# Modulation products in halves of the contraction, at twenty places instead of ten

## What is computed

```python
for l in range(DEPTH):
    mod = (jax.nn.silu(c_ctx) @ ada_w[l] + ada_b[l])[None, None, :]     # ada_w: (2, 1024, 6 * 1024)
    x, st = trunk_layer(x, mod, P, l, None)

def trunk_layer(x, mod, P, l, ctx):
    sh1, sc1, g1, sh2, sc2, g2 = jnp.split(mod, 6, axis=-1)
    h = rms_norm(x, P['norm_mix'][l]) * (1 + sc1) + sh1
    ...                                   # l = 0: even_mixer (mLSTM scan and MLA attention), l = 1: odd_mixer
    x = x + g1 * out
    h = rms_norm(x, P['norm_ffn'][l]) * (1 + sc2) + sh2
    x = x + g2 * hier_moe(h, P, l)
```

## Time and profile before

| | us |
|---|---|
| median of three runs | 1317.55 (1315.46 to 1319.56) |
| the profiled execution | 1329.77 |
| its span | 1327.7 |
| TensorE busy | 1190.6 (90%) |
| VectorE, ScalarE, GpSimd busy | 489.2, 350.7, 115.6 |
| TensorE waits in 100 to 330 us: for `in_ada_w` | 12.7, in 5 waits |
| mean rate from HBM over the span | 263 GB/s |

### The profile page before, as it was taken

One profiled execution on the slowest core, in us unless ns is written; L12 is line 12 of the kernel. 1 busy time (PEld: TensorE's weight loads), 2 busy tenths in 40 slices (PEclk: granted clock), 3 DMA queues, 4 the chain that ended last, 5 costly groups with the idle time before them and its releaser, 6 DMA issues. The chain is left out here.

```text
span 1327.7 us, 17676 instructions
## 1 busy us (share of the span) xinstructions
PE 1190.6 (90%) x6730; PEld 686.5 (52%) x6730; DVE 489.2 (37%) x1074; ACT 350.7 (26%) x750; POOL 115.6 (9%) x142
## 2 busy tenths in 40 slices
PE   5999987998999999878899999899889899988884
PEld 3555563346973333333456555888879533333323
DVE  3004473245261111100555984678832511110014
ACT  2101514245222111110324434442432211111111
POOL 1600000000011111110000000200000111111100
PEclk9899998989989999899998999799989899998897
DMA  9972398773569999997513310010274899999971
GB/s 363 315 290 61 126 327 321 286 287 136 243 244 385 417 412 418 409 404 295 204 64 127 107 52 0 2 34 2 100 261 178 310 374 418 410 414 399 392 282 48
DMA packets 87929, 329.15 MB, mean 248 GB/s; under 512 B 19184, under 2 KB 25498, under 8 KB 66977
## 3 DMA queue, kind: packets, MB, share of 16 engines
q1 hardware_dynamic: 72560, 297.40, 57.7%
q0 software_dynamic: 15280, 30.56, 6.6%
HBM read 320.04 MB, written 29.53 MB: 263 GB/s over the span
## 5 line engine op out<-in xcount | busy, mean ns | idle before, releaser
L1020 PE MATMUL psum<-wide,ring 128*128 128x384 f32 x704 | 241.3, 503 | 4.2 <-ACT wide L1764 1.9
L1020 PEld LDWEIGHTS psum<-wide,ring 128*128 128x128 f32 x704 | 165.7, 239 | 71.6 <-issue 9.7
L1395 PE MATMUL psum<-arena 128*64 128x512 f32 x568 | 157.1, 609 | 15.6 <-DMA arena<-in_moe_w_up 10.0
L1020 PE MATMUL psum<-ring,wide 128*128 128x512 f32 (+2 forms) x336 | 119.6, 515 | 0.0
L2511 DVE TENSOR_TENSOR arena<-arena,psum 128x256 f32<-128x256 f32 x34 | 14.3, 422 | 276.8 <-ACT arena L1921 276.8
L1395 PEld LDWEIGHTS psum<-arena 128*64 128x64 f32 x568 | 50.3, 140 | 116.6 <-issue 115.5
L1921 ACT ACTIVATE arena<-psum 128x256 f32<-128x256 f32 x34 | 13.1, 384 | 309.8 <-PE psum L1395 309.8
L1395 PE MATMUL psum<-ring,arena 128*64 128x512 f32 x320 | 77.9, 643 | 11.1 <-DMA ring<-in_moe_w_up 11.1
L1020 PEld LDWEIGHTS psum<-ring,wide 128*128 128x128 f32 x336 | 59.6, 198 | 53.5 <-issue 52.6
L1395 PE MATMUL psum<-wide,arena 128*64 128x512 f32 x160 | 72.2, 605 | 0.0
L2524 DVE TENSOR_SCALAR arena<-psum,share 128x512 f32<-128x512 f32 x34 | 25.5, 751 | 122.0 <-PE psum L1421 121.9
(11 more groups left out here) (544 smaller groups left out, 1673.4 us busy)
## 6 DMA issues: line engine op xcount, KB each, us to landing
ring<-in_ada_w SPq DMA_DIRECT2D x23, 2048.0 KB, 10.0
arena<-in_moe_w_gate SPq DMA_DIRECT2D x24, 1024.0 KB, 11.7
arena<-in_moe_w_up SPq DMA_DIRECT2D x24, 1024.0 KB, 20.5
arena<-in_moe_w_down SPq DMA_DIRECT2D x24, 1024.0 KB, 23.2
ring<-in_moe_w_gate SPq DMA_DIRECT2D x20, 1024.0 KB, 16.6
ring<-in_moe_w_up SPq DMA_DIRECT2D x20, 1024.0 KB, 19.6
ring<-in_moe_w_down SPq DMA_DIRECT2D x20, 1024.0 KB, 21.4
ring<-in_w_in_odd SPq DMA_DIRECT2D x7, 2048.0 KB, 8.3
```

What stands on the lines that cost most here:

```text
L1020: ins = mm(out, lhs(k), rhs(k), start=(k == 0), stop=(k == n - 1))
L1395: ins = mm(psum[half, 2 + s, :].rearrange("p (w f) -> p w f", w=2), hg[s][:, k, half], gate_up_of(UNITS[q][h], k), start=(k == 0), stop=(k ...
```

## The change

A part's `mod_rows` becomes two jobs, one for each half of the contraction. A half needs one load and frees its slot when it is computed. The four column groups are now four quarters of the output columns (every fourth column, `quarter::4`) in place of two halves times even and odd, with 256 columns a matmul. `mod` sums the two halves in PSUM, with `pick` eight columns wide, in two accumulated steps. ScalarE copies each half by itself. The twenty halves of the ten parts have twenty places, and the last `mod` a further one: new ones are at `tb` 1, at `N2` and `CU` of the scan, at `qf` 0, 2, 4 and 6, and at `pT` (0,4), (1,4), (2,0) and (2,4). The first two parts, ahead of the projections, are split as well.

```diff
 def mods_beside():
-    places = [("N1", 2 * pair, 0) for pair in range(3)] + [("cqT", 0), ("hmT", 0), ("qf", 3), ("qR", 0), ("vv", 0)]
-    places += [("pT", c, h) for c, h in ((0, 0), (1, 0), (1, 4))]
+    places = [("tb", 1), ("N1", 0, 0), ("CU", 0, 0), ("N1", 2, 0), ("N2", 2, 0), ("CU", 2, 0), ("N1", 4, 0), ("cqT", 0), ("hmT", 0)]
+    places += [("qf", h) for h in range(0, MLA_H, 2)] + [("qR", 0), ("vv", 0)]
+    places += [("pT", c, h) for c, h in ((0, 0), (0, 4), (1, 0), (1, 4), (2, 0), (2, 4))]
     parts = MOD_PARTS[MODS_FIRST:]
...
+    halves = [("mod_rows", *part, half) for part in parts for half in range(2)]
+    def at(n):
+        whole = [("mod", *parts[n // 2 - 1])] if n and n % 2 == 0 else []
+        return whole + halves[n:n + 1]
...
 def plan_weights():
     def ada(parts):
-        return [("ada", (l, i, half), ("mod_rows", l, i)) for l, i in parts for half in range(2)]
+        return [("ada", (l, i, half), ("mod_rows", l, i, half)) for l, i in parts for half in range(2)]
...
             def modulate(name, l, i, half=0):
+                b = issue(name, l, i, half) if name == "mod_rows" else issue(name, l, i)
                 if name == "mod_rows":
-                    if (l, i) in MOD_PARTS[1:MODS_FIRST]:
+                    if (l, i) in MOD_PARTS[1:MODS_FIRST] and half == 0:
                         keep_busy(b, 3)
-                    w = [weight("ada", (l, i, half)).rearrange("p (k n) -> p k n", k=4) for half in range(2)]
+                    w = weight("ada", (l, i, half)).rearrange("p (k n) -> p k n", k=4)
                     for k in range(4):
-                        for parity in range(2):
-                            for half in range(2):
-                                at_ = 32 * (2 * parity + half)
-                                ins = mm(b[at_:at_ + 32, :], sil[:, 4 * half + k, :], w[half][:, k, parity::2],
-                                         start=(k == 0), stop=(k == 3), tile_position=(0, at_))
+                        for quarter in range(4):
+                            at_ = 32 * quarter
+                            ins = mm(b[at_:at_ + 32, 0:2 * P], sil[:, 4 * half + k, :], w[:, k, quarter::4],
+                                     start=(k == 0), stop=(k == 3), tile_position=(0, at_))
                     ready(ins)
                 else:
-                    pe.wait_ge(*taken("mod_rows", l, i))
-                    for m in range(4):
-                        ins = mm(b[:, 4 * m:4 * m + 4], mod_rows[:, m * P:(m + 1) * P], pick, start=True, stop=True)
+                    for half in range(2):
+                        pe.wait_ge(*taken("mod_rows", l, i, half))
+                    for m in range(2):
+                        for half in range(2):
+                            at_ = (2 * half + m) * P
+                            ins = mm(b[:, 8 * m:8 * m + 8], mod_rows[:, at_:at_ + P], pick, start=(half == 0), stop=(half == 1))
                     ready(ins)
```

More of the change, by code:

```diff
@@ L93 @@
 C_SEL = C_ROT + ROPE
-C_PLACE = C_SEL + 4
+C_PLACE = C_SEL + 8
 C_HOME = C_PLACE + EXPERTS
@@ L136, in const_table @@
     c[:, C_ROW:C_ROW + 2 * TILES] = row + P * np.arange(2 * TILES)[None, :] - NO_ROW
-    for parity in range(2):
-        for half in range(2):
-            for cond in range(2):
-                c[32 * (2 * parity + half) + cond, C_SEL + 2 * parity + cond] = 1.0
+    for quarter in range(4):
+        for cond in range(2):
+            c[32 * quarter + cond, C_SEL + 2 * quarter + cond] = 1.0
     half, nf = ROPE // 2, ROPE // 4
@@ L188, in plan_jobs @@
     jobs += norm(0)
-    jobs += [(name, l, i) for l, i in MOD_PARTS[:MODS_FIRST] for name in ("mod_rows", "mod")]
+    jobs += [job for l, i in MOD_PARTS[:MODS_FIRST] for job in (("mod_rows", l, i, 0), ("mod_rows", l, i, 1), ("mod", l, i))]
     jobs += [("qT", h) for h in range(4)] + [("kT", h) for h in range(4)]
@@ L1070, in _ @@
             for l, i in MOD_PARTS[:MODS_FIRST]:
-                modulate("mod_rows", l, i)
+                for half in range(2):
+                    modulate("mod_rows", l, i, half)
                 modulate("mod", l, i)
@@ L1147, in _ @@
             for c in range(TILES):
+                beside("tb", c)
                 even_rows("tb", c, w, IN_EVEN - 5 * 512)
@@ L1161, in _ @@
                         two_heads(b, half, lambda h: ST[d][:, tok(h)], lambda h: vN[:, c, h, :])
+                beside("N2", 2 * pair, 0)
                 if sequence:
@@ L1170, in _ @@
                             two_heads(b, half, lambda h: qT[:, h, tok(c)], lambda h: mlC[:, 1, d, h, :])
+                beside("CU", 2 * pair, 0)
                 if moves_on:
@@ L1758, in _ @@
             for l, i in MOD_PARTS[:MODS_FIRST]:
-                mod_row_copy(l, i)
+                for half in range(2):
+                    mod_row_copy(l, i, half)
             act.wait_ge(S("normal"), KD)
@@ L1808, in _ @@
             beside("N1", 0, 0)
+            beside("CU", 0, 0)
             head_squares(0, 1)
-            beside("N1", 2, 0)
-            beside("N1", 4, 0)
+            for place_ in (("N1", 2, 0), ("N2", 2, 0), ("CU", 2, 0), ("N1", 4, 0)):
+                beside(*place_)
             head_squares(2, 2)
@@ L2116, in beside @@
             def beside(*job):
-                for name, l, i in parts_at.get(job, []):
+                for name, *part in parts_at.get(job, []):
                     if name == "mod":
-                        modulation(l, i)
+                        modulation(*part)
             def norm(n):
```

28 lines of the change are left out of this document (13 added, 15 removed).

## The result

| | before | changed |
|---|---|---|
| median of 3 runs, us | 1317.55 (1315.46 to 1319.56) | 1357.08 (1354.15 to 1365.64) |
| profiled execution, us (span) | 1329.77 (1327.7) | 1354.15 (1352.1) |
| start of the first projection, us | 40.18 | 44.39 |
| start of `qR`, us | 249.27 | 269.06 |
| start of the output projection, us | 321.86 | 350.64 |

The ratio is 1.027, with a 95% interval of 1.021 to 1.033 (the two medians alone give 1.030). The prediction was 1310.5 us, range 1303 to 1338: the sign is wrong, and the time lies outside the range. What happened is rival 1, beyond even the worst time that was worked out for it (near 1350).

The account below looks back on a forecast made before the run. TensorE's waits for `in_ada_w` weights (12.7 us) and slow clock (4.2 us) were taken as the bound. Start -1.8, middle -5.2 and attention 0 gave -7.0 us: 1310.5 from 1317.55, range 1303 to 1338 (likeliest case 1304 to 1315).

Parts of the forecast that it names:

- rival 1: All halves: reading at stride four costs a factor of 1.55, 3.1 us a half, total 1330.5 us; chance 0.32.
- The price of a half: TensorE products: a half takes 2.0 us where a whole part takes 3.83, with no price for stride four.
- the fourth load: Start: it lands at 32.5 as before, with only 2.0 us of products left behind it, ending at 34.6 for 36.45.
- The cover of 6 us: Rival 1: of 26 us more in the halves, about 6 us fills waits left above (1.4, 1.2, 4.7 us).
- first projection: Start: earlier halves let it begin sooner than 40.18, held by its own weight until 38.4; -1.8 us.
- wait at the first `mod`, then for data: Scan, first pair: TensorE waits for ScalarE's copy from 168.0 to 169.4, then for data until 171.5.
- end of the scan: Last pair's `N2` ends at 200.7 for 198.7, 2.0 us later, with half a part more done.
- wait at `kpR`: Behind the scan: TensorE waits for ScalarE's copies from 205.4 until 210.1, 4.7 us.
- slow clock behind it: After the wait at `kpR`: 1 us of slow clock on TensorE.
- `qR`: Between scan and attention: begins at 243.8 for 249.3.
- Rival 2: Middle: data waits turn wholly into ScalarE and VectorE waits, scan chain another 3 us late; 1315.5 us; chance 0.17.
- Attention and what follows, 0: From the attention on: no change, with 1.5 us to either side; a gain is kept to the end.

Follow-up runs that it names:

- p1: Changed kernel plus overwritten series of matmuls before one half, differing in stride, column groups and columns; four groups took 1.93, 2.01, 2.93, 3.86 us at strides 1 to 4.
- e1: Changed kernel with its schedule kept, but quarters cut to read the moving operand at stride 2 instead of 4; 1322.05 us, ratio 0.9978 to the kernel before.
- e2: Kernel before, whole parts at old places and loads freed in twos, with the changed kernel's stride-4 matmuls; 1359.56 us, ratio 1.024 to before.
- e3: e1 with ScalarE's `kpT` and fourth-part copies before the squares, VectorE's bias earlier, a `qf` half moved to `hmT`; 1316.31 us, ratio 0.9947 to before.
- e4: e3 without the place between `N1` and `N2` of the second pair, a second place at `cqT` instead; 1314.64 us, ratio 0.9927 to before.

## Why the prediction was wrong, step by step

**The price of a half is the step that failed.** The prediction set two ends for an operand that the trace did not show, nothing and a factor of 1.5 to 1.6, and then said "I take no price, because the nearest row in kind, the same matmul at stride two, pays none". Stride two was near in kind but on the other side of the step: p1 shows nothing paid at 8 bytes and twice the time at 16. Measured is 3.82 us for 2.0 forecast, over 24 halves 43.7 us. Of this 3.1 us are not seen as extra, since two of e1's halves ran at half clock (3.47 and 3.64 us) anyway: 40.5 us of busy time, as the groups show. A further 7.4 us went into cover: the wait at the first `mod` (1.6) went, that at `kpR` fell from 4.7 to 2.9 us, the wait for the fourth load (1.45) went, and smaller ones did. 33.1 us remained at the output projection, and 32.6 us of span.

**Rival 1 was right in mechanism and place, and wrong in size.** Its factor, 1.55, was the mean of a weight load and a VectorE operation, two other readers. The VectorE pair was also read as a clean comparison, which it is not: the slower one, L2841, reads PSUM as well and writes at a stride, and L2784 does neither. The moving operand pays 2.0 at a stride of four. The cover of 6 us was about right (7.4). With a factor of two the prediction itself had worked out "near 1350", and then put the range's end at 1338. For that case it had 40 us more; the runs show 33 against e1. That the result still came out above 1350 is due to the base: 1310.5 held a gain of 7 us of which e1's ratio shows 2.9, and it started from three runs of before, 1315 to 1320 us, where 36 others spread over 1316 to 1334 with medians of 1326. Moved to that base the sum is near the measured time: 1310.5, 33 for the stride, 4.1 of gain that did not come and 8.4 from 1317.55 to 1326 make 1356. Even by its own chances, 0.32 for rival 1, the end of the unknown cost belonged inside.

**What e1 says of the rest of the sum.** Without the stride the forecast can be read term by term:

| step | forecast | e1 |
|---|---|---|
| first projection | -1.8 | -0.9 |
| wait at the first `mod`, then for data | 1.4, and to 171.5 | 1.59, then 1.22 |
| third `N1` | 197.0 | 196.39 |
| end of the scan | 200.7 | 200.2 |
| wait at `kpR` | 4.7 | 4.68 |
| slow clock behind it | 1 | 3.3 |
| `qR` | -5.5 | -3.1 |
| output projection | -7.0 | -4.35 |

The chain through the scan held, place by place, with the new waits where they were named. Part of this agreement is luck. In every profile the first projection starts in a stretch of slow clock, for which the forecast had no term. By the mean granted clock of its first 10 to 12 us I estimate its cost at 3.1 us in before, 1.7 in e1, e2 and e3, 2.7 in e4 and 2.8 in the changed kernel, so it varies without a pattern in the change. At the first `SK` of the scan (160.91 before, 160.79 in e1 with one half more done) e1 stood 2.1 us ahead: 0.9 of the forecast's 1.8 at the first projection, and 1.2 from this shorter stretch. These 1.2 us are also part of e1's 4.35 at the output projection, and no run shows that the change caused them.

Two terms of the forecast were mis-sized. The slow clock behind the 4.7 us wait took in three groups: `mod` 1.88 us for 1.10, a half 3.64 for 2.02, `hmT` 2.41 for 1.53, together 3.3 us. I had put 1. The nearest row, the wait of 4.97 us in the kernel before, gave 1.4 us over the part behind it, so 1 was low even by that row. There the clock was back at 1.00 at about 220.5, 3 us into the part; in e1 it stayed at 0.50 until about 217.6, 8 us behind the end of the wait. At the start I let the fourth load land at 32.5 as before. In all seven other profiles it landed 27.4 to 28.0 us after its issue, against 26.7, and where a half waits for it, in e1, e3 and e4, that half began at 33.5 to 33.8. The halves are not the cause, since e2, with whole parts, has 27.5; nor is an earlier fifth load, since the changed kernel issues it only at 29.17. There is one profile of before to set against them, and the cause stays open.

**Rival 2**, that the waits turn wholly into others, did not hold as told, since the chain through the scan was not 3 us later. But e1's measured ratio, 0.9978 with 1 inside its interval, is near where it stood (0.998, 1315.5 for 1317.55): what it called a growing wait came as slow clock. e3, with its three moves, took the wait and the slow clock away together; the wait itself hung on ScalarE's order, since the half that moved stands behind `kpR` in both kernels.

**Attention and what follows, 0.** From `vv`, e1 took 57.9 us to the output projection (259.57 to 317.51) and before 57.3 (264.56 to 321.86), with one half of 2.0 us more in it, so 1.4 us were hidden, within the 1.5 us of doubt. Of the 4.35 us by which the output projection came sooner in the profile, the runs' ratio gives 2.9 (0.22% of 1326), and its interval takes in none.

## What to carry to other kernels

- Before a product is cut differently, look at the byte step of the operand that streams: a free stride is no evidence for the next larger one. Here, at full clock, 8 bytes were free, 12 cost half as much again, and 16 twice; a cut that keeps two neighbours within 16 bytes (e1) had the same schedule for nothing.
- Freeing a slot sooner removes a wait for a load only until the next engine in the fixed order is late. Read that engine's queue in the same pass: here one copy in ScalarE's order cost a wait of 4.68 us and 3.3 us of slow clock behind it.
- A wait that brings the clock down is priced with all that runs behind it at the lower level, not by its own length. Here that was 3.3 us behind 4.68.
- The absolute time of a forecast stands on the runs of before. Three of them lay within 4 us, and 36 others over 18.

## What the runs showed of the hardware that I had not expected

- TensorE's moving operand in 4-byte elements: 1.93, 2.01, 2.93 and 3.86 us at strides of 1, 2, 3 and 4, and no further step at 8 (2.02 us for 128 columns, where stride 1 took 1.07).
- The price is the same with one, two or four column groups (3.77, 3.82, 3.86 us), though four groups side by side read four operands in the time of one, at stride 1 (1.93 and 1.91 us) and at stride 4 (3.86 and 3.77).
- The price of the stride and that of the lower clock don't add: a half at stride 4 took 3.82 us at a granted clock of 1.00 and 3.87 at 0.53, one at stride 2 took 2.02 at 1.00 and 3.64 at 0.50.
- A weight load at a stride of eight took 1.58 times the dense one, the moving operand 1.9 times. The one is no yardstick for the other.
